# Sample attention by head pairs inside the projection loop, its P.V on the tensor engine, and a later gate sigmoid

## The reference

```
xn = RMSNorm(x)
[q | k | v | glu_in | gates] = xn @ w_in
A: 3 head groups, dilations (1, 4, 16), 8 heads x 64; QK-RMSNorm; softmax over
   the dilated window; the groups' outputs are weighted by their softmax
   denominators, then @ w_attn_out
   sample: the new token reads 128 + 128 + 64 cached rows and its own 3 rows
B: u = glu_a * sigmoid(glu_b); causal depthwise conv (width 31); LayerNorm over
   channels; swish; @ w_conv_out
m = sigmoid(g_A) * A + sigmoid(g_B) * B;  h = x + m @ w_o
out = h + W2 relu(W1 RMSNorm(h))^2
also written: the updated key, value and convolution caches
```

## Time and profile before

| | us |
|---|---|
| median of 3 runs | 1109.07 |
| lowest, highest | 1098.77, 1109.81 |
| the profiled execution | 1107.68 |
| its span, first to last instruction | 1105.8 |
| PE busy | 1022.5 |
| DVE busy | 636.0 |
| ACT busy | 507.1 |
| POOL busy | 161.0 |

### The profile page before, as it was taken

One profiled execution on the slowest core, in us unless ns is written; L12 is line 12 of the kernel. 1 busy time (PEld: TensorE's weight loads), 2 busy tenths in 40 slices (PEclk: granted clock), 3 DMA queues, 4 the chain that ended last, 5 costly groups with the idle time before them and its releaser, 6 DMA issues.

```text
span 1105.8 us, 22024 instructions
## 1 busy us (share of the span) xinstructions
PE 1022.5 (92%) x8334; PEld 991.9 (90%) x8334; DVE 636.0 (58%) x896; ACT 507.1 (46%) x762; POOL 161.0 (15%) x178
## 2 busy tenths in 40 slices
PE   2999999999999999985875999999999999999998
PEld 2899999899899899875874898999999999999998
DVE  3577779568658768758967925554442224443221
ACT  4333367667668558643640234444541114453221
POOL 4000000220220220238255013110000000000000
PEclk8899999999999999998886989999999999999999
DMA  6233585484575556336673432344444444444442
GB/s 175 77 95 91 195 324 164 138 292 147 179 239 193 188 193 218 109 107 234 137 228 99 160 114 72 93 131 140 130 140 143 142 129 131 140 142 143 137 158 67
DMA packets 173010, 169.57 MB, mean 153 GB/s; under 512 B 7850, under 2 KB 162762, under 8 KB 170231
## 3 DMA queue, kind: packets, MB, share of 16 engines
q1 hardware_dynamic: 163271, 138.49, 39.2%
q0 software_dynamic: 9664, 30.08, 8.6%
HBM read 159.19 MB, written 64.86 MB: 203 GB/s over the span
## 4 chain that ended last, share of the span: by engine, by line
PE 77%; ACT 7%; DVE 5%; issue 5%; DMA 3%; SPq 1%; POOL 1%; DVEq 0%; ACTq 0%; POOLq 0%
PE ps L673 68%; DMA w_raw<-in_w_conv_out_dram 2%; PE ps L613 1%; ACT w_high L984 1%; PE ps L600 1%; PE ps L785 1%; DMA chan_rows<-in_norm_g_dram 1%; ACT L907 1%; DVE ln_sum L1377 1%; DVE w_low L1256 1%; PE ps L569 1%; POOL gate_a L1699 1%; PE ps L777 1%; PE ps L587 1%; PE ps L562 1%
## 5 line engine op out<-in xcount | busy, mean ns | idle before, releaser
L1256 DVE TENSOR_TENSOR w_low<-w_raw,w_high 128x1024 fp32r<-128x1024 f32 x152 | 208.0, 1368 | 308.0 <-ACT w_high L984 308.0
L984 ACT ACTIVATE w_high<-w_raw 128x1024 fp32r<-128x1024 f32 x152 | 161.1, 1060 | 424.8 <-PE ps L673 407.9
L673 PE MATMUL ps<-x_high,w_high 128*128 128x260 f32 x1600 | 330.8, 288 | 7.9 <-ACT far_b L972 2.6
L673 PE MATMUL ps<-x_high,w_low 128*128 128x260 f32 x1600 | 323.6, 284 | 0.0
L673 PE MATMUL ps<-x_low,w_high 128*128 128x260 f32 x1600 | 323.4, 284 | 0.0
L673 PEld LDWEIGHTS ps<-x_high,w_high 128*128 128x128 f32 x1600 | 248.3, 190 | 15.6 <-issue 9.8
L673 PEld LDWEIGHTS ps<-x_high,w_low 128*128 128x128 f32 x1600 | 248.2, 190 | 0.0
L673 PEld LDWEIGHTS ps<-x_low,w_high 128*128 128x128 f32 x1600 | 248.0, 190 | 0.0
L1161 DVE SCALAR_TENSOR_TENSOR conv<-u_in,chan,conv x240 | 168.1, 749 | 10.2 <-DVE conv L1161 7.9
L673 PE MATMUL ps<-hid_high,w_high 128*128 128x260 f32 x512 | 103.6, 284 | 0.0
L673 PE MATMUL ps<-hid_high,w_low 128*128 128x260 f32 x512 | 103.1, 283 | 0.0
(11 more groups left out here) (247 smaller groups left out, 1167.6 us busy)
## 6 DMA issues: line engine op xcount, KB each, us to landing
w_raw<-in_w_in_dram SPq DMA_DIRECT2D x68, 512.0 KB, 4.2
w_raw<-in_w_ff_dram SPq DMA_DIRECT2D x64, 512.0 KB, 4.1
out_dram<-in_cache_v_dram SPq DMA_DIRECT2D x64, 256.0 KB, 5.8
out_dram<-in_cache_k_dram SPq DMA_DIRECT2D x64, 256.0 KB, 4.1
out_dram<-in_cache_k_dram SPq DMA_DIRECT2D x8, 1022.0 KB, 7.2
out_dram<-in_cache_v_dram SPq DMA_DIRECT2D x8, 1022.0 KB, 7.0
kbuf<-in_cache_k_dram POOLq DMA_DIRECT2D x2, 2048.0 KB, 14.7
qbuf<-new_qkv POOLq DMA_DIRECT2D x4, 1024.0 KB, 7.1
```

The lines of the kernel that those rows point to most:

```text
L673: mm = pe.matmul(out[:, h, :], w[:, k, n0:n0 + P], x[:, k0 + k, h * HT:(h + 1) * HT], start=(first and k == 0 and n == 0), stop=(last and ...
L984: act.activation(w_high[a % 2][:, :, :], w_raw[a % 2][:, :, :], ACT.Copy).then_inc(cast_done, 1)
L1256: dve.tensor_tensor(w_low[a % 2][:, :, :], w_raw[a % 2][:, :, :], w_high[a % 2][:, :, :].bitcast(F32), ALU.subtract).then_inc(split_done, 1)
```

## The change

- The scores of the sample move into the QKV loop. POOL loads, for the two heads of pass t, 128 channels of the keys of the three caches (`load_keys`) and, once the new rows are stored, of the queries (`load_queries`). DVE multiplies and reduces them in `dots` at the end of the pass, around the split of the last gate unit. The Fori over the four passes on POOL is written out.
- POOL's K and V products and DVE's weighting and adding of V are gone. V of all three groups is loaded after the loop. PE makes P.V after output unit 0: 24 matmuls with 32 stationary columns (8 heads of one request, padded with zeros) and 512 moving columns of V, in four column tiles. DVE keeps of each head's row its own 64 channels (`o_blk`), and 8 matmuls after output unit 2 turn that into `attn`.
- The transposes and the softmax of the sample move into the gate stage: after gate units 2 and 5 on PE, in units 3 and 4 on ACT and DVE.
- The gate tiles of the convolution are copied from PSUM with Copy; Sigmoid follows in the output stage, before DVE's product with the tile.
- The squares of the LayerNorm get eight buffers, and a tree of seven adds in place of a copy and seven adds in a row.
- ACT's table for Ln and Exp together is asked for ahead of the QKV loop, and the one for Ln ahead of the gate stage.
- `o_high` and `o_low` are made once for all columns.

```diff
+SQ_TREE = ((0, 1, 2, 0), (2, 3, 4, 0), (0, 2, 0, 2), (4, 5, 6, 0), (6, 7, 8, 0), (4, 6, 0, 5), (0, 4, 0, 6))
@@ tensor: gate units
                 if j == 3:
-                    pe.wait_ge(csq_sum, KT)
+                    pe.wait_ge(csq_sum, KT - 1)
...
+                if j == 2:
+                    pe.wait_ge(s_red, 2 * NB)
                     pe.wait_ge(centred, KT)
...
+                if j == 5:
                     pe.wait_ge(s_pn, 1)
...
@@ tensor: output units
+                if j == 0:
+                    pe.wait_ge(s_ptc, 2)
+                    pe.wait_ge(v_in[0], 16)
+                    pe.wait_ge(v_in[1], 16)
+                    pe.wait_ge(v_in[2], 32)
+                    for half in range(2):
+                        for g in range(G):
+                            n = SROWS[g]
+                            for b in range(4):
+                                mm = pe.matmul(ps[32 * b:32 * (b + 1), 4 + half, :], s_prob_t[0:n, g, 4 * half + b, :],
+                                               v_tiles[g][0:n, 4 * half + b, :], start=g == 0, stop=g == G - 1)
+                    mm.then_inc(s_pv, 1)
...
-                if j == 6:
-                    pe.wait_ge(v_sum, 5)
-                    pe.wait_ge(mixed, NB)
+                if j == 2:
+                    pe.wait_ge(s_blk, 2)
                     for ct in range(4):
-                        for b in range(TS):
-                            mm = pe.matmul(ps[:, 6, ct * TS + b:ct * TS + b + 1], qbuf[:, b, ct * P:(ct + 1) * P], ones[:, 0:1],
+                        for half in range(2):
+                            mm = pe.matmul(ps[:, 4, ct * TS + 4 * half:ct * TS + 4 * half + 4], o_blk[:, half, ct * P:(ct + 1) * P],
+                                           b_pick[:, :], start=True, stop=True)
@@ scalar
+            act.preload_act_table_set("natural_log_exp_and_others")
             with act.Fori(0, 2) as tt:
...
+            act.preload_act_table_set("natural_log")
...
-                act.activation(ln_sq[:, k % 4, :], conv[:, k, :], ACT.Square).then_inc(csq_done, 1)
+                act.activation(ln_sq[:, k, :], conv[:, k, :], ACT.Square).then_inc(csq_done, 1)
...
-                act.activation(halves(gate_c[:, j, :]), pair(j % 2), ACT.Sigmoid).then_inc(tile_free, 1)
+                act.activation(halves(gate_c[:, j, :]), pair(j % 2), ACT.Copy).then_inc(tile_free, 1)
...
+                    act.wait_ge(s_mx, 1)
+                    act.activation(s_prob[:, :], ps[0:64, 4, 0:SKEYS], ACT.Exp, scale=-1.0, bias=s_small[0:64, 4:5],
...
             for j in range(8):
                 cast(U_COUT + j + 2, 0, 0)
+                act.wait_ge(tile_free, j + 1 + 2)
+                act.activation(gate_c[:, j, :], gate_c[:, j, :], ACT.Sigmoid).then_inc(gate_full, 1)
@@ vector: QKV loop, after the last taps
+            def dots(i, keys, queries, n, key_in, query_in, g0, gn):
+                dve.wait_ge(key_in, cnt(32, 32))
+                dve.wait_ge(query_in, cnt(32, 32))
+                dve.tensor_tensor(keys, keys, queries, ALU.mult).then_inc(kq_done, 1)
+                dve.wait_ge(kq_done, cnt(2, i + 1))
+                to = s_score[0:n, g0:g0 + gn, :].rearrange("p g (b h) -> p (g b) h", h=HEADS)[:, :, bass.ds(tt * 4 + 2 * t2, 2)]
+                dve.tensor_reduce(to, keys.rearrange("p b (h e) -> p b h e", e=E), AX.X, ALU.add).then_inc(s_red, 1)
...
+            dots(0, k01[:, :, :, :].rearrange("p g b c -> p (g b) c"), q01[:, :, :, :].rearrange("p g b c -> p (g b) c"),
+                 P, k01_in, q01_in, 0, 2)
             split(U_QKV + PER_T * t2 + 10 + 2, 2 * PER_T, tt)
+            dots(1, k2[0:SROWS[2], :, :], q2[0:SROWS[2], :, :], SROWS[2], k2_in, q2_in, 2, 1)
@@ vector: gate units
-                        if k == 0:
-                            dve.tensor_copy(ln_sum[:, :], ln_sq[:, 0, :]).then_inc(csq_sum, 1)
-                        else:
-                            dve.wait_ge(csq_sum, k)
-                            dve.tensor_tensor(ln_sum[:, :], ln_sum[:, :], ln_sq[:, k % 4, :], ALU.add).then_inc(csq_sum, 1)
+                        dve.tensor_tensor(ln_sq[:, a, :], ln_sq[:, a, :], ln_sq[:, b, :], ALU.add).then_inc(csq_sum, 1)
...
-                if j >= 2:
-                    sample_scores(dve, (j - 2) // 2, j % 2)
...
+                if j == 4:
+                    dve.wait_ge(s_exp, 1)
+                    dve.reciprocal(s_small[0:64, 7:8], s_small[0:64, 6:7]).then_inc(s_rs, 1)
+                    dve.wait_ge(s_rs, 1)
+                    dve.tensor_scalar(s_prob[:, :], s_prob[:, :], s_small[0:64, 7:8], None, ALU.mult).then_inc(s_pn, 1)
@@ gpsimd: QKV loop
+            def load_keys(t):
+                col = slice(t * P, (t + 1) * P)
+                for g in range(2):
+                    pool.dma_start(k01[:, g, :, :], cache_tile(cache_k, g)[:, :, col]).then_inc(k01_in, 16)
+                pool.dma_start(k2[0:64, :, :], cache_tile(cache_k, 2)[:, :, col]).then_inc(k2_in, 16)
...
                     pool.dma_start(scratch[n][:, :, col], new_tok[:, n, :, :]).then_inc(new_stored, 16)
+                pool.wait_ge(new_stored, 48 * t + 48)
+                load_queries(t)
                 pool.wait_ge(gate_copied, 2 * t + 4)
...
+                if t < 3:
+                    pool.wait_ge(s_red, 2 * (t + 1))
+                    load_keys(t + 1)
@@ gpsimd: after the loop (the products and the K loads are removed)
             pool.wait_ge(tb_free, 2 + 4 * TB_PER_T)
+            pool.dma_start(kbuf[:, :, :], cache_tile(cache_v, 0)).then_inc(v_in[0], 16)
             pool.dma_start(qbuf[:, :, :], cache_tile(cache_v, 1)).then_inc(v_in[1], 16)
+            pool.wait_ge(s_red, 2 * NB)
+            pool.dma_start(kbuf2[0:64, :, :], cache_tile(cache_v, 2)).then_inc(v_in[2], 16)
```

More of the change, by code:

```diff
@@ L379, in build_step @@
         o_low_done = sem("o_low_done")
[L381 to L382 removed]
+        k01_in = sem("k01_in")
+        k2_in = sem("k2_in")
+        q01_in = sem("q01_in")
+        q2_in = sem("q2_in")
         kq_done = sem("kq_done")
@@ L741, in _ @@
                 if j == 3:
-                    pe.wait_ge(csq_sum, KT)
+                    pe.wait_ge(csq_sum, KT - 1)
                     pe.wait_ge(ut_copied, 1)
                     for h in range(2):
-                        mm = pe.matmul(ps[:, 6 + h, 0:HT], ones[:, :], ln_sum[:, h * HT:(h + 1) * HT], start=True, stop=True)
+                        mm = pe.matmul(ps[:, 6 + h, 0:HT], ones[:, :], ln_sq[:, 0, h * HT:(h + 1) * HT], start=True, stop=True)
                     mm.then_inc(var_done, 1)
[L749 to L753, removed]
+                if j == 2:
+                    pe.wait_ge(s_red, 2 * NB)
                     pe.wait_ge(centred, KT)
@@ L768, in _ @@
                     mm.then_inc(s_ptr, 1)
+            for j in range(8):
+                unit(U_COUT + j, 0, 0, tile(8 + j, 0, 0), c_high, c_low,
+                     ready=(lambda k: pe.wait_ge(c_low_done, k + 1)) if j == 0 else None).then_inc(unit_done, 1)
+                if j == 0:
[10 more added lines that the diff above has]
+                    mm.then_inc(s_pv, 1)
                 if 1 <= j <= NB:
@@ L1581, in _, with load_queries @@
             pool.memset(c_sum[:, :, :], 0.0).then_inc(c_summed, 1)
-            pool.dma_start(kbuf2[:, :, :], cache_tile(cache_k, 0)).then_inc(k_in, 16)
-            with pool.Fori(0, 4) as t:
+            qrow, krow, vrow = scratch[0], scratch[1], scratch[2]
+            def load_keys(t):
[3 more added lines that the diff above has]
+                pool.dma_start(k2[0:64, :, :], cache_tile(cache_k, 2)[:, :, col]).then_inc(k2_in, 16)
+            def load_queries(t):
+                at, step = qrow.offset + t * P, G * AW
+                for g in range(2):
+                    pool.dma_start(q01[:, g, :, :], bass.AP(qrow.tensor, at + g * AW, [[0, P], [step, TS], [1, P]])).then_inc(q01_in, 16)
+                pool.dma_start(q2[0:64, :, :], bass.AP(qrow.tensor, at + 2 * AW, [[0, 64], [step, TS], [1, P]])).then_inc(q2_in, 16)
+                col = slice(t * P, (t + 1) * P)
+                pool.dma_start(q2[64:67, :, :], qrow.rearrange("b g c -> g b c")[:, :, col]).then_inc(q2_in, 16)
+                pool.dma_start(k2[64:67, :, :], krow.rearrange("b g c -> g b c")[:, :, col]).then_inc(k2_in, 16)
+            load_keys(0)
+            for t in range(4):
                 col = bass.ds(t * P, P)
```

191 lines of the change are left out of this document (69 added, 122 removed).

## The result

| | before | after |
|---|---|---|
| median of 4 runs | 1106.47 us | 1071.7 us |
| lowest, highest | 1098.77, 1109.81 | 1068.59, 1074.17 |
| the profiled execution | 1107.68 | 1070.58 |

The ratio is 0.9675 with a 95% interval of 0.964 to 0.9709: 34.8 us less, where 43.1 were forecast.

What follows compares the result with a forecast made beforehand. PE was taken as the bound, with waits and a low clock from 480.92 us; its stretch summed to 125.0 us against 168.1, 43.1 less, so 1107.7 - 43.1 = 1064.6 us, range 1053 to 1082.

Steps and rivals of the forecast that it cites:

- 2, channel sums, means, unit behind: Gate stage start: channel sums stay on POOL; PE's wait, the means and the slower unit behind cost 7.1 us.
- 3, small matmuls: PE's stretch from the first gate unit: u_in transposes, score transposes and variance take 2.3 us.
- V burst ("Nothing taken"): Gate stage: 5 MB of V ahead of a weight load, taken as mostly drained; 0 us, 11.3 as the bound.
- 5, s_pn, transposes, slow units: After the sixth gate unit: PE idles 3.7 us for normalised probabilities, then transposes and a slow restart; 5.6 us together.
- 7, P.V: Sample P.V on PE: 24 matmuls on four 32-column tiles, taken as four abreast, 6.1 us.
- 8, selection, last step: Output stage: head selection stays at 7.6 us; the last step falls to 8 narrow matmuls, 2.6 us.
- 4 and 6: Gate and output stages: the 15.5 us wait for the LN sum and the 4.2 us of c_low waits go.
- Moved into the QKV loop: DVE's dots (28 us) hidden, key, query and V loads at nothing, fewer table loads gaining 0 to 2 us.
- the rival with 0.06: V burst holds one weight load as long as before, all behind the cast slips 11.3 us: 1075.9 us; chance 0.06.
- the 2 us the prediction allowed: Sign in the profile: PE's start in the gate stage within 2 us of 480.9; later means keys or queries.
- QKV pays for the keys' bytes: Rival in the QKV loop: key loads delay weight loads, up to 12 us, time up to 1076.6; chance 0.11.
- The queries' rival: QKV loop: DVE's dots wait for late queries and PE behind them, 13.5 us each, 1118.6 us; chance 0.03.

Runs made afterwards that it cites:

- e10_best: Changed kernel with V in pieces, probability transposes after gate unit 6, keys loaded late in each pass, state copy and new rows' stores behind the merge's loads: 1057.13 us.
- e11_sum_early: POOL's channel sums put ahead of the stores of the attention statistics in each pass, against e10_best: 1051.8 us.

## Why the prediction was right, and where it was off

The direction and the mechanism held. In PE's stretch, from the first gate unit's start (476.67) to the last output unit's end (593.09 + 3 x 5.855 = 610.65), 134.0 us were measured where 125.0 were summed:

| step | summed | measured | difference |
|---|---|---|---|
| 2, channel sums, means, unit behind | 7.1 | 4.7 | -2.4 |
| 3, small matmuls | 2.3 | 2.0 | -0.3 |
| V burst ("Nothing taken") | 0 | 7.6 wait + 2.3 slow unit | +9.9 |
| 5, s_pn, transposes, slow units | 5.6 | 4.0 + 0.6 + 2.6 | +1.6 |
| 7, P.V | 6.1 | 5.3 | -0.8 |
| 8, selection, last step | 2.6 | 1.9 | -0.7 |
| the unit behind step 8 | 0 | 7.37 - 5.86 | +1.5 |

That makes 8.8 of the 9.0; the rest is rounding and units at 5.95.

- **What carried the forecast: POOL's products hold DVE.** Shown from both sides: taking them out of the kernel before gives back 28.7 us, putting products into the changed one (with V in pieces) costs 12 and stretches four adds to 9.21 us. The steps that rest on it (4 and 6: no wait for the LN sum, none for c_low) came as written; the tree was done at 504.1, ahead of PE.
- **The step that failed: the V loads in "Moved into the QKV loop".** It said that the burst would be mostly drained when the next weight load was issued, and took nothing, with 21.7 us of the earlier trace rows as the bound. The load took 21.9 us: the bound was the value. At the 331 GB/s that the prediction used for the keys, 5 MB take 15.8 us. By its own times (V from 492, the load at 502.3) a third of the burst was then still to come, so "mostly drained" was too much. But this division alone does not give the stall: V and the load behind it would have been in by 509.4, ahead of the 512.6 needed; with the measured issue times it gives 504.2, where the load was needed by about 510 (PE asked at 512.4, and cast and split take 2.4). In the run V was in at 508.6 and the load 9 us later; from 505 to 508 the DMA engines moved only 246 GB/s at a share of 1.13. So what failed is the overlap: the load did not get through beside the burst and what else was issued, and the full-stretch rate did not hold for the mix. Why it didn't stays open; with the state copy and the new rows' stores moved away, the load still took 16.4. This was the rival with 0.06, the load held as long as before; it cost 9.9 (7.6 and a slow unit) where the rival had 11.3. V in pieces has a span of 1061.8, and the forecast's own is 1062.7 (1064.6 less the 1.9 around a span): without this step the sum held, in part because the smaller errors of the table cancel, which is luck.
- **Where the time stands otherwise.** The stretch began 4.2 us earlier than in the profile of before, outside the 2 us the prediction allowed. `far_b`, which starts it, lies at 479.8, 478.8 and 476.4 in the kernel before and its two variants, and between 475.5 and 480.3 in the changed kernel and the variants that keep its loop. The two ranges overlap, each value is of one execution, and no gain can be claimed from them. Behind the stretch 458.25 us follow where 456.8 did. With 9.0 more in the stretch, 4.2 less ahead and 1.4 more behind, the span comes out 6.2 above the 1062.7. Why the tail is 1.4 longer stays open.
- **Two sizes in the loop were wrong and cancelled, by luck.** The keys were taken at nothing and the table loads at 0 to 2 us. The common table is worth 7.4 to 9.3 us in the changed kernel and 3.7 in the one before; the keys' bytes are worth 4.4 to 6.5 without it, and nothing measurable with it. ACT's waits up to 475 us show that the keys hold the weight loads even in the changed kernel, where PE doesn't feel it (before: 2.9 us in 3 waits; with keys late and the common table, in `e10_best`: none):

```profile
ACT w_high L1011 <- DMA w_raw<-in_w_in_dram: 36.4, 10, 5.9
```

  The rival "QKV pays for the keys' bytes" would have held for a part of its 12 us had the table not been changed with them.
- **DVE's dots were hidden**, as forecast. The queries' rival, the one on the slower side, stayed away: one wait of 2.0 us in eight, and PE didn't feel it.

```profile
DVE k L1270 <- DMA q<-new_qkv: 2.0, 1, 2.0
```

- **Step 5, s_pn,** was the new wait that the prediction named, 4.0 for 3.7. The slow restart was read as 1.5 and measured 2.6, over three units. In the changed kernel this wait also comes after the burst's; in the kernel with V in pieces it is 3.6.
- **Step 7, P.V:** the extension of the pair row to four tiles held, and 5.3 is below the 6.1 taken, below which I had thought nothing likely. It holds for this order of the matmuls alone.
- **Step 8:** the price scaled with the number of narrow matmuls, but the slow unit behind them did not go, against "units of 7.21 and more become 5.86". Granted clock in that unit:

```profile
576.00:580.00 4.00, 4.00 (x22) 4.00 (x22) 1.05 (x2) 0.00 (x0) 0.00 (x0) 0.57 0.44 125
```

  0.57 is close to the lower level of 1.2 GHz for most of it. This unit took 7.14 to 8.47 in nine of the ten profiles of the changed kernel and its variants, and 5.87 in the tenth (`e11_sum_early`), so the loss is frequent and not certain. Ahead of it PE had done sixteen records of narrow matmuls in 1.88 us, where before 64 took 10.50 with a unit of 7.21 behind the earlier trace rows: a quarter of the narrow work left the same slow unit.
- **Slips in the working.** Step 5's time on ACT adds up to 516.2, not 516.9, and step 4's PE asks at 512.8, not 512.7. Neither changes the sum: DVE's next split waits for unit five's end (519.4) either way.

## What to carry to other kernels

When transfers are moved, divide their bytes by the rate of a full stretch in the trace and look at which small, urgent load is issued in that time. Take the result as the earliest end only: here it gave 502.6 for V, and V was in at 508.6 and the urgent load at 517.5. What helped was to put the large loads in pieces behind the urgent ones, on the same queue. A wait of PE is worth its length and a restart (here 3.6 us were worth 5 to 7, and 2.6 worth 4.5), so moving a short dependent step by one unit, or the work of one engine ahead of its stores, can pay as much as a rewrite. Price two edits that use the same slack together: each alone may be free and the two not.

## What the runs showed that I had not expected

- One weight load of 512 KB on SP's queue, issued 7 us behind 5 MB on POOL's, took 21.9 us; in the company of 1 MB pieces on its own queue such loads took 4.3.
- Twenty-four matmuls of 32 stationary and 512 moving columns took 5.29 us with the four column tiles in turn and 8.91 with three in a row on each; the serial estimate of the prediction was 22.9. The Trainium skill, "TensorEngine Tiling (Array Packing)", "Theoretical Speedup", gives up to 4x for such tiles; 22.9 / 5.29 is 4.3, so the estimate was somewhat high. By the order of the matmuls the same work is 1.7 times as long here.
- Behind eight narrow matmuls (1.88 us) the next unit ran at a granted clock of 0.57 for 4 us, and at full clock in one variant (`e11_sum_early`, 5.87 us).
- Between 505 and 508 us the DMA engines showed a share of 1.13 and moved 246 GB/s; between 405 and 416 in the kernel before it was 0.93 and 331. A full share says little about the rate of a mix.
